# Five probability tiles, and one transposition step a slot, in an attention loop of a hybrid decoder

## The reference

```python
h = rms_norm(x, norm_g[l])
proj = jnp.einsum('btd,dc->btc', h, w_in[l])
y_a = nsa_mixer(q_a, kv_a, g_a, ...) * jax.nn.silu(z_a)   # 16 heads of 64, 2 key groups
y_b = fox_mixer(q_b, k_b, v_b, f_b, b_forget[l]) * jax.nn.silu(z_b)   # 16 heads of 64
merged = (jax.nn.sigmoid(r_a) * jnp.einsum('btc,cd->btd', y_a, w_proj_nsa[l])
          + jax.nn.sigmoid(r_b) * jnp.einsum('btc,cd->btd', y_b, w_proj_fox[l]))
x = x + jnp.einsum('btd,de->bte', merged, w_out[l])
```

## Time and profile before

| | us |
|---|---|
| median of 3 runs (1458.53 to 1458.86) | 1458.62 |
| the profiled execution | 1458.66 |
| its span in the trace | 1456.9 |
| PE busy | 1441.6 (99%) |
| DVE / ACT / POOL busy | 1030.2 / 906.7 / 491.4 |
| eight cycles of the first layer, about | 108 to 522 |
| merge and output stage behind them | 522 to 739 |

### The profile page before, as it was taken

The page is one execution under the profiler, slowest core; times in us unless marked ns, Lnnn a source line. Parts: engine busy times, 40 slices in busy tenths (PEclk is TensorE's granted clock), DMA queues, the critical chain, the costliest instruction groups (busy, mean ns, idle before and its releaser), DMA issues.

```text
span 1456.9 us, 22913 instructions
## 1 busy us (share of the span) xinstructions
PE 1441.6 (99%) x7490; PEld 1223.3 (84%) x7490; DVE 1030.2 (71%) x2431; ACT 906.7 (62%) x1912; POOL 491.4 (34%) x578
## 2 busy tenths in 40 slices
PE   9999999999999999999999999999999999999998
PEld 7888888888888888888888888888888888888887
DVE  6837888888888874444576488888888887643444
ACT  6636888778878752223364487788788887522234
POOL 2403664555556420000022155554565555000000
PEclk9999999999999999999999999999999999999999
DMA  9232212212122143333453321212122121433332
GB/s 284 75 101 59 58 47 57 59 45 59 45 59 53 51 130 92 96 101 90 111 184 89 101 53 51 59 44 59 47 57 58 45 58 46 144 92 104 92 101 91
DMA packets 201627, 118.29 MB, mean 81 GB/s; under 512 B 9305, under 2 KB 195889, under 8 KB 201009
## 3 DMA queue, kind: packets, MB, share of 16 engines
q1 hardware_dynamic: 199120, 107.49, 27.1%
q0 software_dynamic: 1728, 8.66, 1.6%
q10 hardware_dynamic: 672, 0.83, 0.2%
HBM read 110.54 MB, written 6.42 MB: 80 GB/s over the span
## 4 chain that ended last, share of the span: by engine, by line
PE 84%; ACT 6%; DVE 4%; issue 4%; POOL 1%; DVEq 0%; POOLq 0%; ACTq 0%
PE acc L1888 54%; PE turned L1962 6%; PE o_pair L1987 6%; PE scores L1945 3%; PE scores L1947 3%; PE turned L2214 2%; ACT q_fox L891 2%; PE scores L2214 1%; ACT prob L963 1%; ACT w_hi L842 1%; PE turned L2138 1%; DVE prob L1447 1%; PE misc L2007 1%; DVE q_fox L1359 1%; PE scores L1888 1%
## 5 line engine op out<-in xcount | busy, mean ns | idle before, releaser
L1888 PE MATMUL acc<-u_lo,w_hi 128*128 128x512 f32 x968 | 380.1, 393 | 0.0
L1888 PE MATMUL acc<-u_hi,w_hi 128*128 128x512 f32 x968 | 379.4, 392 | 0.0
L1888 PE MATMUL acc<-u_hi,w_lo 128*128 128x512 f32 x968 | 378.8, 394 | 0.0
L1272 DVE TENSOR_TENSOR w_lo<-w_raw,w_hi 128x1024 fp32r<-128x1024 f32 x184 | 231.1, 1256 | 126.8 <-ACT w_hi L842 125.8
L963 ACT ACTIVATE prob<-prob,row_max 128x384 f32<-128x384 f32 (+3 forms) x384 | 215.3, 561 | 119.7 <-DVE row_max L1447 113.8
L842 ACT ACTIVATE w_hi<-w_raw 128x1024 fp32r<-128x1024 f32 x184 | 193.4, 1052 | 151.4 <-PE acc L1888 95.3
L765 POOL TENSOR_SCALAR prob<-prob,row_inv,gates 128x256 f32<-128x256 f32 (+3 forms) x256 | 184.0, 720 | 215.1 <-DVE row_inv L1454 214.4
L1888 PEld LDWEIGHTS acc<-u_hi,w_lo 128*128 128x128 f32 x968 | 182.0, 188 | 34.0
L1888 PEld LDWEIGHTS acc<-u_hi,w_hi 128*128 128x128 f32 x968 | 181.8, 188 | 33.5 <-issue 0.2
L1888 PEld LDWEIGHTS acc<-u_lo,w_hi 128*128 128x128 f32 x968 | 181.9, 188 | 32.1 <-issue 0.2
L1447 DVE CUSTOM_DVE_ANT_0 prob<-scores,causal 128x384 f32<-128x384 f32 (+3 forms) x384 | 184.4, 480 | 19.2 <-PE scores L1947 18.2
(11 more groups left out here) (330 smaller groups left out, 2562.9 us busy)
## 6 DMA issues: line engine op xcount, KB each, us to landing
w_raw<-in_w_in_dram SPq DMA_DIRECT2D x140, 512.0 KB, 3.7
w_raw<-in_w_proj_nsa_dram SPq DMA_DIRECT2D x16, 512.0 KB, 3.8
w_raw<-in_w_proj_fox_dram SPq DMA_DIRECT2D x16, 512.0 KB, 3.8
w_raw<-in_w_out_dram SPq DMA_DIRECT2D x16, 512.0 KB, 3.8
x_scratch<-xT POOLq DMA_DIRECT2D x2, 2048.0 KB, 8.7
xT<-x_scratch POOLq DMA_DIRECT2D x2, 2048.0 KB, 8.8
x_nat<-in_x_dram SPq DMA_DIRECT2D x4, 512.0 KB, 6.5
c_w<-in_cmp_w_k_dram SPq DMA_DIRECT2D x4, 512.0 KB, 5.5
```

Of the source, the lines that this page charges most:

```text
L1272: dve.tensor_tensor(w_lo[:, par, :, 0:width], w_raw[:, par, :, 0:width], w_hi[:, par, :, 0:width], ALU.subtract).then_inc(w_lo_done, 1)
L1888: ins = pe.matmul((bank or acc[par])[0:width, :], own_w, rhs, start=(n == 0), stop=(n == 23))
```

## The change

The ring of probability tiles becomes five, the fifth being `v_raw`, and is counted over all steps of the kernel, not within a part of a cycle. `both` goes. In its place every slot transposes one step, three slots old (`turn_lags`), ACT makes its upper part in the same slot and DVE its lower part a slot later (`low_lags`); the value matmuls of a step come five slots after it and the narrow ones six. The planner counts the costs by the new lags, so the distribution of projection matmuls and the units' ends move: the inner cycles' ends of the units 0 to 4 are slots 5, 10, 14, 19, 23 (before 4, 8, 13, 18, 23), the last cycle's 6, 11, 18, 24, 28 (before 4, 10, 16, 23, 27), with 29 slots for 28. Slots that had been written with `LAG_PV` are now numbers of the same value. One semaphore, kf_first, is now raised by the second copy of kf_hi and not by the first.

The diff, context left out:

```diff
@@ -54,13 +54,12 @@
-SM_RING = 4
+SM_RING = 5
...
-LAG_SCALE, LAG_TURN, LAG_PT, LAG_PV = 1, 2, 3, 4
-LAG_NARROW = LAG_PV + 2
+LAG_SCALE, LAG_PV = 1, 5
@@ -78,9 +77,19 @@
-def both(s, lag):
-    return (lag + 1, lag) if (s - lag) % 2 else ()
+def turn_lags(s):
+    return (3,)
+def low_lags(s):
+    return (4,)
+def narrow_lags(s):
+    return (6,)
@@ -95,8 +104,8 @@
-            for lags, cost in (((-1,), self.score_cost), (both(s, LAG_TURN), self.turn_cost),
-                               (both(s, LAG_PV), self.value_cost)):
+            for lags, cost in (((-1,), self.score_cost), (turn_lags(s), self.turn_cost),
+                               ((LAG_PV,), self.value_cost)):
@@ -225,7 +234,7 @@
-        sb("up_to_2_kb", [P, 32])
+        sb("up_to_2_kb", [P, 29])
@@ -283,7 +292,7 @@
-            prob = sb("prob", [P, SM_RING, T])
+            prob = sb("prob", [P, SM_RING - 1, T])
@@ -488,6 +497,10 @@
+        def prob_of(ring):
+            return v_raw if ring == SM_RING - 1 else prob[:, ring, :]
@@ -753,9 +766,9 @@
-                (a, qt), ring = pair.at(s), s % SM_RING
+                (a, qt), ring = pair.at(s), (pair.s0 + s) % SM_RING
...
-                p = prob[:, ring, 0:P * (qt + 1)]
+                p = prob_of(ring)[:, 0:P * (qt + 1)]
@@ -777,7 +790,7 @@
-                at(CYCLE_STEPS + 1 if cycle.last else 16 + LAG_PV + 3, lambda: gate_output(cycle.nsa))
+                at(CYCLE_STEPS + 1 if cycle.last else 23, lambda: gate_output(cycle.nsa))
@@ -899,7 +912,7 @@
-                        if h == 0 and rows == own(0):
+                        if h == 0 and rows == other(0):
@@ -958,9 +971,9 @@
-                    ring, width = s % SM_RING, P * (pair.at(s)[1] + 1)
+                    ring, width = t % SM_RING, P * (pair.at(s)[1] + 1)
...
-                    act.activation(prob[:, ring, 0:width], prob[:, ring, 0:width], ACT.Exp,
+                    act.activation(prob_of(ring)[:, 0:width], prob_of(ring)[:, 0:width], ACT.Exp,
@@ -979,9 +992,9 @@
-                    at(LAG_PV + 1, lambda: lower_half(before, 1))
-                at(8 + LAG_PV + 1, lambda: lower_half(nsa, 0))
-                at(16 + LAG_PV + 1, lambda: lower_half(nsa, 1))
+                    at(5, lambda: lower_half(before, 1))
+                at(13, lambda: lower_half(nsa, 0))
+                at(21, lambda: lower_half(nsa, 1))
@@ -1008,7 +1021,7 @@
-                    for lag in both(s, LAG_TURN):
+                    for lag in turn_lags(s):
@@ -1437,20 +1450,20 @@
-                    t, qt, ring = pair.s0 + s, pair.at(s)[1], s % SM_RING
+                    t, qt, ring = pair.s0 + s, pair.at(s)[1], (pair.s0 + s) % SM_RING
...
-                    dve.tensor_tensor_reduce(prob[:, ring, 0:width], scores[bank][:, first:first + width],
+                    dve.tensor_tensor_reduce(prob_of(ring)[:, 0:width], scores[bank][:, first:first + width],
...
-                    ring = s % SM_RING
+                    ring = (pair.s0 + s) % SM_RING
@@ -1469,9 +1482,9 @@
-                    at(LAG_PV + 2, lambda: head_output(before, 1))
-                at(8 + LAG_PV + 4, lambda: head_output(nsa, 0))
-                at(16 + LAG_PV + 2, lambda: head_output(nsa, 1))
+                    at(6, lambda: head_output(before, 1))
+                at(16, lambda: head_output(nsa, 0))
+                at(22, lambda: head_output(nsa, 1))
@@ -1518,7 +1531,7 @@
-                    for lag in both(s, LAG_PT):
+                    for lag in low_lags(s):
@@ -1960,7 +1973,7 @@
-                                           prob[:, s % SM_RING, P * kt:P * kt + P], ident[:, :])
+                                           prob_of((pair.s0 + s) % SM_RING)[:, P * kt:P * kt + P], ident[:, :])
@@ -2025,21 +2038,21 @@
-                def ending(s, lag):
-                    for n in (s - each for each in both(s, lag)):
-                        now = cycle.step(n) if n < CYCLE_STEPS else None
+                def ending(s, lags):
+                    for lag in lags:
+                        now = cycle.step(s - lag) if s - lag < CYCLE_STEPS else None
...
-                    if ending(s, LAG_PV):
-                        extra.setdefault(s, []).append(lambda now=ending(s, LAG_PV): value_step(*now))
+                    if ending(s, (LAG_PV,)):
+                        extra.setdefault(s, []).append(lambda now=ending(s, (LAG_PV,)): value_step(*now))
...
-                    return ending(s, LAG_NARROW)
+                    return ending(s, narrow_lags(s))
@@ -2048,7 +2061,7 @@
-                    turns = [cycle.step(s - lag) for lag in both(s, LAG_TURN) if s < plan.slots and s - lag < CYCLE_STEPS]
+                    turns = [cycle.step(s - lag) for lag in turn_lags(s) if s < plan.slots and s - lag < CYCLE_STEPS]
```

## The result

| | before | after |
|---|---|---|
| median, us (5 runs each) | 1458.58 (1458.38 to 1458.86) | 1512.72 (1511.69 to 1514.11) |
| ratio | | 1.0371, 95% interval 1.0357 to 1.0385 |
| span of the profiled execution | 1456.9 | 1511.0 |

The changed kernel is 54 us slower. The forecast was 1492, with 1458 to 1508 as its range: the direction was right, the time lies 4.7 us above the range. Lines of the bodies have moved by 13 (L1888 is L1901, L1962 is L1975).

The account below looks back on a forecast made before the run. PE (TensorE) was taken to bound all stages. Inner cycles 2.5 + 0.7 - 0.6 = 2.6, x 12 = 31.2, first cycles 2.5, last 0: 1458.7 + 33.7 = 1492 us, range 1458 to 1508 (8 in 10).

Parts of the forecast that it names:

- PE's own content unchanged: On PE, same number of transposes, scores and projection matmuls; splitting the runs costs 0, bounds 0 to 0.4 us a cycle.
- The old stall of 0.31: Inner cycle, at 440.81: two transposes take 0.70 instead of 0.39 because GpSimd is late; claimed to go.
- the other (0.29): Inner cycle, at 436.36: transposes of step 6 wait for step 4's lower part to leave the PSUM bank; 0.29 us lost.
- The rival with one tile's spacing more for each run: Worse: each of 12 more runs a cycle costs 0.11 us for an unhidden weight load, 21 us in all: 1513; chance 0.05.
- First chain: From slot 5: q_fox and pc_t back to back delay step 7's transposes to 12.6 us against PE's 10.1; 2.5 us lost.
- The first cycles: First cycle of each layer: no y_all in slot 6, so 1.8 + 0.7 - 1.24 = 1.3 us more each, x 2 = 2.5.
- Second chain: From slot 14: VectorE's w_lo, kf_lo and q_raw in slot 15 delay step 14's transposes to 6.85 against 6.17; 0.7 us lost.
- the waits of transposes for GpSimd gone: Sign of being right: PE's transposes no longer wait for GpSimd's scaling, as they run two slots after it.
- A third place near slot 23: Inner cycle, where q_nsa's lower part comes one slot later: cost taken as 0, at most 0.3 us.
- The bounds for an inner cycle: Net loss of an inner cycle, 2.6 us with 0.5 off or on twice: 1.7 to 3.6, giving 1480 to 1505 us.
- Last cycles: Last cycle of each layer: another plan, one slot more and shorter slots; taken as 0, between -1.65 and +3 us each.
- Rival (2), faster: All old stalls between PE's matmuls go and none comes: 1458.7 - 13 = 1446 us; chance 0.14.

Follow-up runs that it names:

- E11: Changed kernel with an even hand-written distribution (inner ends 4, 8, 13, 19, 23), fox gate a slot earlier, last cycle distributed as in the kernel before: 1459.12 us, 1.0003.
- E4: Changed kernel with pc_t's copy on ScalarE and its part on VectorE each a slot later (8 and 9): 1493.55 us, 1.0238.
- E7: Changed kernel with the second half of kf (ScalarE's rounding, VectorE's lower part) a slot earlier: 1510.3 us, 1.0359.
- E6: Changed kernel with the fox gate's tanh (ScalarE) and product (VectorE) a slot earlier, unit 3's end plus 3 and 4: 1510.13 us, 1.0356.
- E9: Changed kernel with eight extra 512-column matmuls in slot 10 of first and inner cycles, in the 2 us stop, results overwritten: 1506.11 us, 1.0325.
- E5: Changed kernel with the kernel before's projection-matmul distributions written out for inner and last cycles; new lags and five tiles stay: 1461.52 us, 1.002.
- E12: E11 with the last cycle also distributed evenly (ends 4, 10, 16, 23, 28): 1456.02 us against 1458.75, ratio 0.9982.
- E3: Changed kernel with a ring of four probability tiles in place of five: 1511.81 us, 1.0362.
- E1: Changed kernel with the planner counting transposes and values by the old pairs; new lags and ring of five stay: 1472.53 us, 1.0096.
- E8: Changed kernel with an even hand-written inner distribution (ends 4, 8, 13, 18, 23), last cycle distributed as in the kernel before: 1464.74 us, 1.004.
- E10: Changed kernel with E4, E6 and E7 together: 1487.26 us, 1.0195.

## Why the prediction was right in sign and wrong in size

1. **PE's own content unchanged: right.** Merging takes 217.0 for 216.8. An inner cycle of E11 without its stop takes 50.37, one of before without its 0.6 takes 50.27: by this estimate 0.1 for twelve more runs, within the 0 to 0.4 given. The old stall of 0.31 is absent there, as forecast; near the place of the other (0.29) a stop of 0.18 is left. The rival with one tile's spacing more for each run (1.3 us a cycle) is out.
2. **First chain: right.** Forecast 12.6 us against PE's 10.1, a loss of 2.5 with the part at step 5; measured 12.70 and 2.37 (0.39 and 1.98). E4 takes pc_t's 0.86 out of it and wins 1.04. The first cycles came out at 1.5 for 1.3.
3. **Second chain: right.** 6.85 and 7.03, loss 0.7 and 0.82. E7 moves one term of it, and the stop goes. The sign "the waits of transposes for GpSimd gone" came out the other way in the view of waits (26.2 and 7.7 us under its name, for 2.4 and 0.8): the prediction had allowed for the later of the releasers, and the view names the one that was done first.
4. **"A third place near slot 23 ... take it as 0, at most 0.3": failed.** It is 0.68 a cycle, and it was another term than the one I looked at (q_nsa's lower part): the gate's tanh, tied to unit 3's end, which came behind the exponential of step 23. E6 removes it. The bounds for an inner cycle held even so (3.35 within 1.7 to 3.6), but this is most of the 9 us by which twelve of them exceed the forecast.
5. **The clock: left out, the second step that failed.** I priced a stop by its length. No row of before had a stop this long inside a cycle, and none showed half clock there; the sum had no term for it, and neither had a rival or the range. It is 6.2 us in the changed kernel, shown by E9, and without it the time would have been 1506.5, within the range.
6. **"Last cycles ... I take 0, between -1.65 and +3 each": the size was off.** 2.3 each, within the bounds. E5 loses 1.9 there under before's distribution, so the new lags can cost that much without any moved end; E12 takes 1.5 off what E11 loses, and the stops there fall by as much, so most of that cost comes of the new lags together with a distribution made for pairs. The changed kernel's own stops there add up to some 2.8 us for 1.6 before, so about 1.2 of the 2.3 are waits; the rest, and the 0.7 that E12 keeps, I have not traced.
7. **Rival (2), faster.** Its mechanism exists: with the ends back in place and the matmuls spread evenly the old stalls go but for a stop of 0.18, and E12 is faster. It won 2.7 us, not the 13 at most: 0.33 an inner cycle rather than 0.6, since that stop and some 0.1 for the runs are left.

The sum of the errors: 9.0 (inner cycles) + 6.2 (clock) + 4.6 (last) + 0.5 (first) = 20.3, and 1492.4 + 20.3 = 1512.7.

## What to carry to other kernels

A planner's costs are part of the schedule: when a lag changes, list every piece tied to a moved end, on every engine, and look for each at what now stands behind it; pieces at fixed slots (pc_t) are where it collides. A stop of a full TensorE can cost more than its length (here up to 1.56 us more), so look at the granted clock behind each stop, and price a fix with the clock free to move: E6 and E7 removed real stops and won almost nothing. When an order is changed, compare it with the old distribution held still (E5) before judging it: here the order itself cost 3 us and the plan that came with it 51. And look at the first and last turns of a loop by themselves: E4 and E6 gave back there a part of what they won in the others.

## What the runs showed of the hardware

- After stops of about 2 us in a PE that is else busy, the granted clock fell to half for 3.41 us, 1.56 us longer for the cycle (1.22 in E7). Not every such stop did it: 4 of 12 inner cycles after, 8 with E6, 7 with E7, and with equal stops in other cycles (E3). In E1 each last cycle has two such stops (2.5 and 2.3), and half clock follows the first alone. E4, E5, E8, E10, E11 and E12 had no stop of 2 us and no half clock in their cycles. Eight matmuls in the stop (E9) removed it. Which of the stops are followed by it stays open.
- Of two things that a wait needs, the profile named GpSimd's scaling, done 4 us earlier, and not VectorE's lower part, which had just ended. With the lower part at the same place in E4 it named that one.
- A run of one to four transposes costs PE by the tile: twelve more runs in a cycle came to some 0.1 us (an estimate from 50.37 in E11 and 50.27 before, stops taken out).
